# Gated delta rule in a hybrid decoder step: the two chunks of a tile exchanged for heads 2 and 3

## The reference, cut to what matters

```python
def _gated_delta_chunk(S, q, k, v, g, beta):
    gc = jnp.cumsum(g, axis=-1)
    ...
    a_mat = jnp.where(strict, beta[..., :, None] * decay * kk, 0.0) + jnp.eye(L)
    eg = jnp.exp(gc)
    rhs = beta[..., None] * (v - eg[..., None] * (k @ S))
    u = triangular_solve(a_mat, rhs, lower=True, unit_diagonal=True)
    qk = jnp.einsum('bhid,bhjd->bhij', q, k) * decay
    o = eg[..., None] * (q @ S) + qk @ u
    w_last = jnp.exp(gc[..., -1:] - gc)
    S_new = jnp.exp(gc[..., -1])[..., None, None] * S + einsum('bhjd,bhj,bhje->bhde', k, w_last, u)
    return S_new, o

S, o = lax.scan(lambda c, t: _gated_delta_chunk(c, *t), S, xs)   # xs: chunks of 64 tokens
```

## Time and profile before

| | |
|---|---|
| median of 3 runs | 3388.72 us (3386.82 to 3389.07) |
| the profiled execution | 3394.18 us |
| its span, first to last instruction | 3392.4 us |
| mean granted TensorE clock | 0.988 |
| PE busy | 3318.4 us, 98% |
| DVE busy | 1986.6 us, 59% |
| ACT busy | 1491.5 us, 44% |
| instructions of the state product and of the output product | 128 each (256 records each) |

### The profile page before, as it was taken

The page is one execution under the profiler, slowest core; times in us unless marked ns, Lnnn a source line. Parts: engine busy times, 40 slices in busy tenths (PEclk is TensorE's granted clock), DMA queues, the critical chain, the costliest instruction groups (busy, mean ns, idle before and its releaser), DMA issues. The chain is left out here.

```text
span 3392.4 us, 59846 instructions
## 1 busy us (share of the span) xinstructions
PE 3318.4 (98%) x24010; PEld 2937.5 (87%) x24010; DVE 1986.6 (59%) x3789; ACT 1491.5 (44%) x3027; POOL 396.3 (12%) x369
## 2 busy tenths in 40 slices
PE   8899999999999999999999999999999999999998
PEld 7877889999998877899998877889898877789897
DVE  6744435543547654586666744577575855478484
ACT  4324334221234544454553644455353644446362
POOL 3111000342513110000003101000000311000000
PEclk9889999999999999999999999999999999999999
DMA  4201013565743111344563211245464211246452
GB/s 158 63 27 59 32 51 108 189 228 173 254 176 110 58 42 49 111 152 146 159 199 108 71 39 51 86 145 169 136 205 136 69 46 45 69 124 187 121 181 97
DMA packets 142817, 392.51 MB, mean 116 GB/s; under 512 B 18288, under 2 KB 20288, under 8 KB 139072
## 3 DMA queue, kind: packets, MB, share of 16 engines
q1 hardware_dynamic: 142544, 388.69, 35.4%
HBM read 353.95 MB, written 35.69 MB: 115 GB/s over the span
## 5 line engine op out<-in xcount | busy, mean ns | idle before, releaser
L612 DVE TENSOR_TENSOR wl<-raw,wh 128x512 fp32r<-128x512 f32 (+1 forms) x795 | 750.9, 952 | 596.5 <-ACT wh L605 592.2
L605 ACT CAST wh<-raw 128x512 fp32r<-128x512 f32 (+1 forms) x795 | 636.0, 808 | 465.5 <-PE bank L872 385.7
L872 PE MATMUL bank<-xnT,wh 128*128 128x512 f32 (+2 forms) x2432 | 721.8, 380 | 7.6 <-ACT gate L1608 5.5
L872 PE MATMUL bank<-hnT,wh 128*128 128x256 f32 (+2 forms) x3016 | 580.6, 290 | 3.1 <-ACT V L1870 3.1
L872 PEld LDWEIGHTS bank<-xnT,wh 128*128 128x128 f32 x2432 | 428.9, 191 | 79.9 <-issue 12.9
L872 PEld LDWEIGHTS bank<-hnT,wh 128*128 128x128 f32 x3016 | 473.5, 188 | 8.5 <-ACT V L1870 3.7
L872 PE MATMUL bank<-hid,wh 128*128 128x512 f32 (+1 forms) x1760 | 467.5, 353 | 0.0
L872 PE MATMUL bank<-xnT,wl 128*128 128x512 f32 (+2 forms) x1280 | 460.2, 363 | 0.0
L872 PE MATMUL bank<-hnT,wl 128*128 128x256 f32 (+2 forms) x1508 | 437.2, 290 | 0.0
L872 PE MATMUL bank<-Tm,wh 128*128 128x256 f32 x2016 | 368.6, 282 | 1.1 <-ACT sg L1870 1.0
L872 PEld LDWEIGHTS bank<-hid,wh 128*128 128x128 f32 x1760 | 309.5, 188 | 45.8
(11 more groups left out here) (360 smaller groups left out, 4770.2 us busy)
## 6 DMA issues: line engine op xcount, KB each, us to landing
raw<-in_wstream SPq DMA_DIRECT2D x346, 512.0 KB, 3.5
raw<-wsum SPq DMA_DIRECT2D x252, 256.0 KB, 3.4
raw<-in_wstream SPq DMA_DIRECT2D x189, 256.0 KB, 2.7
ops_in<-in_wstream SPq DMA_DIRECT2D x44, 512.0 KB, 7.7
wsum<-ops_out SPq DMA_DIRECT2D x22, 1024.0 KB, 6.4
hT<-in_xT SPq DMA_DIRECT2D x4, 2048.0 KB, 9.1
out_yp_out<-hT SPq DMA_DIRECT2D x16, 512.0 KB, 2.9
xr<-in_x_prompt SPq DMA_DIRECT2D x12, 512.0 KB, 7.3
```

Of the source, the lines that this page charges most:

```text
L605: act.copy(hi_cell(n), raw_cell(n)).then_inc(sem("hi_done"), 1)
L612: nc.vector.tensor_tensor(lo_cell(n), raw_cell(n), hi_cell(n).bitcast(F32), ALU.subtract).then_inc(sem("lo_done"), 1)
L872: ins = nc.tensor.matmul(*a, **k)
```

## The change

In every tile of 128 prompt tokens, heads 2 and 3 hold the two chunks in exchanged halves of the partitions: chunk 0 of heads 0 and 1 lies in rows 0 to 63, chunk 0 of heads 2 and 3 in rows 64 to 127. `chunk_half(x, k)` is the half of head x in chunk k. The recurrence still runs chunk 0 of all heads, then chunk 1 of all heads. What follows from that:

- the exchange is made where the tokens come in: the SiLU of the channel blocks of heads 2 and 3 writes two instructions of 64-column pieces in place of one (`conv_silu`), and the decay and beta inputs of heads 2 and 3 are read from the other half of the partitions (three small instructions in place of one, four in group 0);
- it is undone where the output rows are copied: two ACT copies of two heads each in place of one of four;
- the state product and the output product take the heads in the order 0, 2, 1, 3; the state product writes heads 0 and 1 to bank 3 and heads 2 and 3 to bank 7 (k = 0) or bank 1 (k = 1); the output product stays in one bank;
- WS and the updates of S take the heads in the same order, and u is formed on all 128 partitions.

```diff
+        PAIRS = ((0, 2), (1, 3))
+        HALVES = ((slice(0, CH), slice(CH, P)), (slice(CH, P), slice(0, CH)))
+        chunk_half = lambda x, k: k if x < NH // 2 else 1 - k
...
                     for k in range(P // CH):
                         e = 2 * t + k
-                        rs = slice(CH * k, CH * (k + 1))
                         ob = (1, 5)[k]
-                        other = slice(CH * (1 - k), CH * (2 - k))
+                        half = lambda r: slice(CH * r, CH * (r + 1))
+                        dsb = (3, (7, 1)[k])
                         claim(ob, "ob_rd", F + e + 1)
-                        for x in range(NH):
-                            pe.wait_ge(*made("S_done", NH * (F + e - 1) + x + 1))
-                            last = nc.tensor.matmul(bank[ob][:, P * x:P * (x + 1)], WQ[:, x, P * k:P * (k + 1)], S[:, x, :],
-                                                    start=x == 0, stop=False, skip_group_check=True)
+                        for q, x in enumerate((*PAIRS[0], *PAIRS[1])):
+                            r = chunk_half(x, k)
+                            pe.wait_ge(*made("S_done", NH * (F + e - 1) + q + 1))
+                            last = nc.tensor.matmul(bank[ob][:, P * x:P * (x + 1)], WQ[:, x, P * r:P * (r + 1)], S[:, x, :],
+                                                    start=q == 0, stop=False, skip_group_check=True)
                         last.then_inc(sem("WS_ps"), 1)
                         if k == 1 and t + 1 < NT:
                             delta_rows(t + 1)
                         beside(t, 14 + 2 * k)
                         pe.wait_ge(*made("u_done", F + e + 1))
-                        claim(3, "S_done", NH * (F + e + 1))
-                        for x in range(NH):
-                            last = nc.tensor.matmul(bank[3][:, P * x:P * (x + 1)], kw[rs, x, :], u[rs, x, :], start=True, stop=True)
+                        for b in dsb:
+                            claim(b, "S_done", NH * (F + e + 1))
+                        for pair in PAIRS:
+                            for b, x in zip(dsb, pair):
+                                rs = half(chunk_half(x, k))
+                                last = nc.tensor.matmul(bank[b][:, P * x:P * (x + 1)], kw[rs, x, :], u[rs, x, :], start=True, stop=True)
                         last.then_inc(sem("dS_ps"), 1)
-                        for x in range(NH):
-                            last = nc.tensor.matmul(bank[ob][other, P * x:P * (x + 1)], QK[rs, x, :], u[rs, x, :],
-                                                    start=False, stop=True, skip_group_check=True)
+                        for pair in PAIRS:
+                            for x in pair:
+                                r = chunk_half(x, k)
+                                last = nc.tensor.matmul(bank[ob][half(1 - r), P * x:P * (x + 1)], QK[half(r), x, :], u[half(r), x, :],
+                                                        start=False, stop=True, skip_group_check=True)
                         last.then_inc(sem("o_ps"), 1)
...
-            act.activation(beta[:, sl, :], ab[:, sl, NH:], ACT.Exp, scale=-1.0).then_inc(sem("act_g"), 1)
+            act.activation(beta[:, sl, 0:2], ab[:, sl, NH:NH + 2], ACT.Exp, scale=-1.0)
+            if first:
+                act.activation(beta[:, 0, 2:], ab[:, 0, NH + 2:], ACT.Exp, scale=-1.0)
+            for dst, src in HALVES:
+                ins = act.activation(beta[dst, 1:, 2:], ab[src, 1:, NH + 2:], ACT.Exp, scale=-1.0)
+            ins.then_inc(sem("act_g"), 1)
...
+            def conv_silu(j):
+                if j % NH < NH // 2:
+                    return act.activation(post[:, j, MAIN], cy[j % 2][:, MAIN], ACT.Silu)
+                dst = post[:, j, MAIN].rearrange("p (t r c) -> p t r c", r=2, c=CH)
+                src = cy[j % 2][:, MAIN].rearrange("p (t r c) -> p t r c", r=2, c=CH)
+                act.activation(dst[:, :, 0], src[:, :, 1], ACT.Silu)
+                return act.activation(dst[:, :, 1], src[:, :, 0], ACT.Silu)
...
-                    act.copy(o_rows[0:CH], bank[1][CH:, :].rearrange("p (h e) -> p h e", h=NH)).then_inc(sem("ob_rd"), 1)
+                    o_bank = bank[1][:].rearrange("p (h e) -> p h e", h=NH)
+                    act.copy(o_rows[0:CH, 0:2], o_bank[CH:, 0:2])
+                    act.copy(o_rows[0:CH, 2:], o_bank[0:CH, 2:]).then_inc(sem("ob_rd"), 1)
...
-            link(v_.tensor_tensor(tg2[:, sl, :], ab[:, sl, 0:NH], bh(p("dtb"), [P, nsl, NH]), ALU.add))
+            dtb = bh(p("dtb"), [P, NT + 1, NH])
+            step(v_.tensor_tensor(tg2[:, sl, 0:2], ab[:, sl, 0:2], dtb[:, sl, 0:2], ALU.add))
+            if first:
+                step(v_.tensor_tensor(tg2[:, 0, 2:], ab[:, 0, 2:NH], dtb[:, 0, 2:], ALU.add))
+            for dst, src in HALVES:
+                step(v_.tensor_tensor(tg2[dst, 1:, 2:], ab[src, 1:, 2:NH], dtb[src, 1:, 2:], ALU.add))
+            settle()
...
-                        v_.tensor_tensor(u[rs], U0[rs], bank[(1, 5)[k]][rs, :].rearrange("p (h e) -> p h e", h=NH), ALU.subtract).then_inc(sem("u_done"), 1)
+                        v_.tensor_tensor(u[:], U0[:], bank[(1, 5)[k]][:].rearrange("p (h e) -> p h e", h=NH), ALU.subtract).then_inc(sem("u_done"), 1)
...
-                        for x in range(NH):
-                            v_.scalar_tensor_tensor(S[:, x, :], S[:, x, :], egl[:, x, k:k + 1], bank[3][:, P * x:P * (x + 1)], ALU.mult, ALU.add).then_inc(sem("S_done"), 1)
+                        for pair in PAIRS:
+                            for b, x in zip((3, (7, 1)[k]), pair):
+                                r = chunk_half(x, k)
+                                v_.scalar_tensor_tensor(S[:, x, :], S[:, x, :], egl[:, x, r:r + 1], bank[b][:, P * x:P * (x + 1)], ALU.mult, ALU.add).then_inc(sem("S_done"), 1)
```

More of the change, by code:

```diff
@@ L1687, in scalar @@
                     act.wait_ge(*made("conv_y", j))
-                    act.activation(post[:, j - 1, MAIN], cy[(j - 1) % 2][:, MAIN], ACT.Silu).then_inc(sem("conv_post"), 1)
+                    conv_silu(j - 1).then_inc(sem("conv_post"), 1)
                     if first:
@@ L1707, in scalar @@
             act.wait_ge(*made("conv_y", NCONV))
-            act.activation(post[:, NCONV - 1, MAIN], cy[(NCONV - 1) % 2][:, MAIN], ACT.Silu).then_inc(sem("conv_post"), 1)
+            conv_silu(NCONV - 1).then_inc(sem("conv_post"), 1)
             if first:
@@ L1780, in delta @@
                     act.wait_ge(*made("o_ps", F + 2 * t + 2))
-                    act.copy(o_rows[CH:], bank[5][0:CH, :].rearrange("p (h e) -> p h e", h=NH)).then_inc(sem("ob_rd"), 1)
+                    o_bank = bank[5][:].rearrange("p (h e) -> p h e", h=NH)
+                    act.copy(o_rows[CH:, 0:2], o_bank[0:CH, 0:2])
+                    act.copy(o_rows[CH:, 2:], o_bank[CH:, 2:]).then_inc(sem("ob_rd"), 1)
                     act.wait_ge(*made("ob_rd", F + 2 * t + 2))
```

## The result

The changed kernel takes 3367.47 us (median of 5 runs, 3365.04 to 3372.75), the kernel before 3388.72 in the same series (5 runs, 3383.41 to 3398.45). The ratio is 0.994, with a 95% interval of 0.9924 to 0.9955: faster by 21.2 us. A second series gave 3367.60 against 3389.17 (ratio 0.9944, 0.9931 to 0.9958). The forecast was 3364, its range 3355 to 3374.

What follows compares the result with a forecast made beforehand. PE, busy 98% of the span, was taken as the bound. Terms -27.9 + 1.6 + 0.8 + 0.7 = -24.8 us, taken from the median 3388.7, gave 3364 us (3363.9), range 3355 to 3374.

Steps and rivals of the forecast that it cites:

- the two products: State and output product pair across row halves, 0.65 and 0.58 us per chunk, saving 27.9 us over 32 chunks.
- wait for S between the chunks: WS of chunk 1 waits for the updates of S, 0.1 us in each of 16 tiles: 1.6 us, ends 0 and 4.0.
- gate wait: Two output copies take 0.07 us more than one, paid at 12 tile ends: 0.8 us, ends 0 and 2.6.
- start of group 0: Extra small ACT and DVE instructions lengthen the decay's chain that PE waits for: 0.7 us, ends 0 and 2.
- Case A: The forecast itself: both products run their halves side by side, 3354.5 to 3373.7 us; 85%.
- U's sixteen records: U (L1305), alternating halves, does sixteen records in 1.02 us; the output product (L1357) needs 1.01 us for eight.
- The line drawn between L1300 and L1068: State product's pace at 128 columns, interpolated between 64- and 256-column rows: 0.088 us each, 0.70 us.
- Rival B: PE lets one half at a time write a bank, so only the state product gains: 3377.7 us; 6%.
- C: Each change of row half costs what entering and leaving a product costs, adding 34.6 us: 3426 us, slower; 3%.
- D: Nothing runs side by side in the two products, only the additions count: 3391.8 us, no measurable change; 6%.
- Neighbouring products: PE's pace in the two products was read from rows whose neighbouring products lie in different row halves.
- In the other groups the convolution's products stand in front: Outside group 0, the convolution's products were to cover the longer decay chain at the group's start; costed at 0.

Runs made afterwards that it cites:

- kernel with single instructions: Changed kernel with decay and beta inputs formed in single instructions again, heads 2 and 3 taking those of the wrong chunk; one run, 3364.51 us.
- kernel with the earlier exponentials: Changed kernel plus gate copy before the cast at tile ends, earlier decay arguments, and beta's exponentials ahead of the wait for VectorE's sums; 3360.97 us, again 3360.94 us.

## Why the prediction was right, and where it was not

| term | predicted, us | measured, us | from |
|---|---|---|---|
| the two products | -27.9 | -27.4 | 32 x (0.445 + 0.41) |
| wait for S between the chunks | 1.6 | 0.2 | WS 1.01 instead of 1.00, 16 times; the output product's 0.02 in front of WS is in the row above |
| gate wait | 0.8 | 2.7 | 5.5 to 8.2 |
| start of group 0 | 0.7 | 0.3 | 26.87 instead of 26.58; not shown to be the edit's |
| convolution's start, groups 1 to 3 | 0 | 3.0 | from start to start; idle 0.72 + 0.94 + 0.58 |
| sum | -24.8 | -21.2 | medians: -21.2 and -21.6 |

**Case A held**, by the step that carried it: U's sixteen records in the time of eight stood for a pairing that the output product has too. Counting steps (four of 0.109 and the ends) gave 0.65 and 0.58 us, measured 0.645 and 0.585; the kernel with three heads in a half confirmed the count at a third point. The line drawn between L1300 and L1068 (0.70) was the worse estimate.

**Rival B fell** with the output product at 0.59 us in one bank. The Trainium skill, "TensorEngine Tiling (Array Packing)", section "Gotcha 1: PSUM Pressure", rules out access of two row tiles to one bank at a time; the trace doesn't agree for this product, whose halves write different partitions. C and D fell with the same rows.

**"Neighbouring products"** was one word too many: the prediction ascribes the pace to neighbours in different halves, and so to the order of heads that the change writes. The order gives nothing that shows; the exchange of the chunks gives all.

**The wait for S** was sized from an update that ends 1.93 us behind the state product's start and a fourth product of WS at 1.88. The lateness stayed near 0.03 us a tile (0.02 ahead of WS, 0.01 in it), near the lower end.

**The gate wait** failed in its size. The queue was named rightly. The row that I took the overlap from copies 128 partitions out of two banks, these copy 64 out of two halves of one bank and overlap hardly at all: 0.17 us instead of 0.07. The 0.13 between the cast and the gate copy was not in the sum at all, and the count was off: nine tile ends, not twelve. That the upper end (2.6, as 16 x 0.16) lies next to the measured 2.7 (9 x 0.30) is luck.

**The start of group 0** was luck too. The products do start 0.74 us later, but 0.45 of it PE brought along, and the remaining 0.3 is there without the extra instructions as well. No run shows what they cost there.

**"In the other groups the convolution's products stand in front"** is the step that failed. It named a cover without measuring its length. In group 3 the chain grew by 1.69 us (9.25 to 10.94) and PE waited 0.58: there had been 1.1 us to spare, and the rest became a wait, in each of the three groups. The term that stood at 0 came to 3.0 us, and the kernel with single instructions has none of it.

## What to carry to other kernels

Products with half of the rows can be laid in both halves, and then cost what the fuller half costs; balance the halves, and don't spend work on the order inside a product, but keep products of one kind together. A cover has a length: before an edit behind it is costed at nothing, measure how late the covered chain ends, and how much the edit adds with its neighbours on the other engines. Where an engine's order is changed to cure a wait, do it only where the moved step's input is ready by then, or it holds up what stands behind it.

## What the runs showed of the hardware

- Products of one row half run beside products of the other half that are written before them (heads 2 and 3 behind 0 and 1: 0.65 us, as in the alternating order), but not across the border of the two products (2.46 us instead of 1.26).
- Two row halves write one bank side by side where they write different partitions of it: the output product takes 0.59 us with two heads in each half, 0.80 with three and one, 1.01 with four in one.
- A second copy of 64 x 256 out of the other half of a bank starts 0.38 us after the first, where a pair of 128 x 256 out of two banks starts 0.27 apart.
- Short steps of VectorE can end with a step of another engine: the same step on 128 x 16 took 0.28 us when it began 4.93 us behind the copy and 0.83 when it began 4.38 behind it, with POOL in its rotations of 128 x 320 (0.88 us each). In both cases the next POOL step began 0.06 us behind the end of that VectorE step. POOL's timeline of the kernel with the earlier exponentials, whose step ended at 2605.79:

```profile
2604.89 0.88 POOL L1969 TENSOR_TENSOR qkv<-rt,rt 128x320 f32<-128x320 f32 x1
2605.85 0.88 POOL L1970 TENSOR_TENSOR rt<-qkv,rope_t 128x320 f32<-128x320 f32 x1
```

  The Trainium skill, "Trainium Architecture — The Big Picture", section "What this means for kernel authors", says that VectorE and GpSimd share a pair of ports under an exclusive lock. The 0.83 us agree with that; no run here took POOL's work away to show it.
